# Two feed-forward down products: from eight block products a tile to seven, with the operand sums on GpSimd

## The chip, the cores and the metric

One Trainium2 chip, one of its cores. The metric is the device time of one launch in microseconds. All numbers are float32.

## The reference

A transformer of two blocks on 256 tokens of width 1024. The first block has two layers (one with a gated delta rule, one with sparse attention), each followed by a gated feed-forward part:

```
h   = rms_norm(x, norm_ffn_w[i])
u   = h @ ffn_w_up[i]                       # 1024 -> 2 x 2816, gate half and value half
g   = silu(causal_dwconv(u[gate], ffn_conv_w[i]) + ffn_conv_b[i]) * u[value]
x   = x + g @ ffn_w_down[i]                 # 2816 -> 1024: the down product
```

The second block has two layers with a mixer and a mixture of 32 experts. Before them, the modulations `silu(c) @ w_ada + b_ada` are computed: 24 chunks of 1024x512, spread through the first block.

## The kernel before

Each engine has its own instruction stream, written as one Python function, and the engines meet at semaphores (`wait_ge`, `then_inc`). Weights come through a ring `W` of six slots of 2 MB (128 partitions x 4096 values), filled in a fixed order by the SP queue: a fill waits until the slot's last reader has released it (`W.free`). PSUM is eight banks of 128x512 in two rings of four, `PA` and `PB`; a bank is taken in ring order, and the taker waits until its last reader has freed it.

The up product already uses seven block products in place of eight (`product(i, part)`, parts 1, 2, 7, 5, 6, 3, 4). Its weight sums run on VectorE (`up_sums`, `own_sums`), 128x1024 each, and write to the slot in place or to the ring `SUMS`.

The down product multiplies `G` (2816 features as 22 blocks of 128, each with 256 tokens) by the down weights. They come as six tiles: tile j > 0 holds blocks 4(j-1) to 4(j-1)+3, tile 0 the blocks 20 and 21, in the order `DOWNS = (1, 0, 2, 3, 4, 5)`. Function `down` (L764) keeps four sums in the four banks of `PA`, one for each half of the tokens (m) and each half of the columns (c), and adds every block with one 128x512 product: 16 products for a tile of four blocks. The last two tiles are one group, which finishes bank after bank, so that the residual `add_x` and the norm of the first half of the tokens start while TensorE does the second.

Between the groups TensorE does modulation sums `ada_sum(n)` (L804 on): one 128x512 product with a matrix of ones, into a bank of `PB`. It needs the chunk that VectorE has weighted and added up (`ada_chunk(n)`, L1817: one `tensor_scalar` and seven `scalar_tensor_tensor` of 128x512, all in the weight slot); VectorE then reads the bank (`ada_out(n)`). `ADA_DOWN` says which chunks stand behind which group: seven in layer 0, six in layer 1. In VectorE's stream chunk n comes ahead of the result n-1, and `add_x` follows the last result.

GpSimd issues a few DMAs in this part and does no arithmetic before the rotary embeddings of the second block.

Of the kernel before, what the change touches and what calls it, by code (L numbers as in the profile page):

```python
# [296 lines left out]
def build(nc, t, out):  # L297
# [34 lines left out]
    slots = [dma(f"w{i}") for i in range(NSLOT + 4)]  # L332
# [13 lines left out]
    def at(n, *shape):  # L346
        k = int(np.prod(shape))
        assert n + k <= ARENA, n + k
        return shaped(AR[:, n:n + k], shape)
# [41 lines left out]
    def tok(m):  # L391
        return slice(m * 128, m * 128 + 128)
# [126 lines left out]
    def blocks(place, kt, n):  # L519
        return place[:, 0:kt * n].rearrange("p (k n) -> p k n", k=kt)  # L520
# [21 lines left out]
    ADA_DOWN = [[(2,), (3, 4), (5, 6), (7, 8)], [(18,), (19,), (20, 21), (22, 23)]]  # L542
    ADA_NSA = [(), (9,), (10,), (11,), (12,)]
    ADA_MIX = {"v": 13, "aq": 14, "av": 15}
    DOWNS = (1, 0, 2, 3, 4, 5)

    def up_name(layer, i):
        return ("up", layer) + UPS[i]
# [154 lines left out]
    def tensor(e):  # L703
# [60 lines left out]
        def down(done, tag, srcs, lhs, between=(), then=None, ready=(), halfway=None):  # L764


            groups = [[x] for x in srcs[:-2]] + [srcs[-2:]]
            for n, group in enumerate(groups):
                held = [(weights(name, kt, 1024), k0, kt) for name, k0, kt in group]
                final = n == len(groups) - 1  # L770
                for m in range(2):
                    if n == 0 and m and halfway:
                        halfway()
                    for c in range(2):
                        if n == 0:
# [359 lines left out]
        def ffn(layer):  # L1135

            done, vect = sig("ffn_mm"), sig("ffn_v")
            tag = ("ffn", layer)

            def product(i, part):  # L1140
                name, nb = up_name(layer, i), up_blocks(i)
                a11, a12, a21, a22, total = up_tiles(layer, i)
                if part == 1:
                    bank(e, PB, ("p1", name))
                    place(name)
                    lhs, rhs, to = a11, HT[:, 0:4, tok(0)], (PB["p1", name], 0)
                    e.wait_ge(sig("norm_ha"), (tag, 0, 3))
                elif part == 2:
                    bank(e, PA, ("p26", name))
                    lhs, rhs, to = a12, HT[:, 4:8, tok(0)], (PA["p26", name], 0)  # L1150
                    e.wait_ge(sig("norm_ha"), (tag, 0, 7))
                elif part == 7:
                    bank(e, PA, ("p57", name))
                    lhs, rhs, to = a21, TS[2], (PA["p57", name], nb)
                    e.wait_ge(vect, ("t", layer, 2))
                    e.wait_ge(vect, ("s3", name))
                elif part == 5:
                    lhs, rhs, to = total, TS[0], (PA["p57", name], 0)
                    e.wait_ge(vect, ("t", layer, 0))
                    e.wait_ge(vect, ("s1", name))  # L1160
                elif part == 6:
                    lhs, rhs, to = a11, TS[1], (PA["p26", name], nb)
                    e.wait_ge(vect, ("t", layer, 1))
                    e.wait_ge(vect, ("s2", name))
                elif part == 3:
                    bank(e, PA, ("p34", name))
                    lhs, rhs, to = a12, HT[:, 4:8, tok(1)], (PA["p34", name], 0)
                    e.wait_ge(sig("norm_ha"), (tag, 1, 7))
                    e.wait_ge(vect, ("s4", name))
                else:  # L1170
# [12 lines left out]

            for i, part in ((0, 1), (0, 2), (1, 1)):
                product(i, part)
            norm_half(tag, 1)
            for i, part in ((1, 2), (2, 1), (0, 7), (0, 5), (0, 6), (0, 3), (0, 4), (1, 7), (1, 5), (1, 6)):
                product(i, part)
            PA.defer()
            product(1, 3)  # L1190
            product(1, 4)
            for i in range(2, 12):
                for part in (1, 2, 7, 5, 6, 3, 4)[i == 2:]:
                    product(i, part)
                if i - 1 in ADA_UP[layer]:
                    ada_sum(ADA_UP[layer][i - 1])

            srcs = [(("down", layer, j), 4 * (j - 1) if j else 20, 4 if j else 2) for j in DOWNS]
            ready = [(vect, ("val", layer, j - 1 if j else 5)) for j in DOWNS]
            down(done, tag, srcs, G, [lambda ns=ns: [ada_sum(n) for n in ns] for ns in ADA_DOWN[layer]],  # L1200
                 None if layer else "nsa", ready)

        def nsa():
            done, vect, act = sig("nsa_mm"), sig("nsa_v"), sig("nsa_a")
# [504 lines left out]
    def vector(v):  # L1709
# [107 lines left out]
        def ada_chunk(n):  # L1817
            done = sig("ada_v")
            name = ("ada", n)
            wt = blocks(W[name], 8, 512)  # L1820
            acc = wt[:, 0, :]
            v.wait_ge(slots[W.where[name]], name)
            v.wait_ge(sig("ada_a"), "c")
            v.tensor_scalar(acc, acc, CC[:, 0:1], None, MUL).then_inc(done)
            for k in range(1, 8):
                v.scalar_tensor_tensor(acc, wt[:, k, :], CC[:, k:k + 1], acc, MUL, ADD).then_inc(done, n if k == 7 else None)
# [299 lines left out]
        def ffn(layer):  # L2126
# [94 lines left out]
            last_results(11)  # L2221
            used(11)
            first, last = ADA_DOWN[layer][0][0], ADA_DOWN[layer][3][-1]
            for n in range(first, last + 2):
                if n <= last:
                    ada_chunk(n)
                if n > first:
                    ada_out(n - 1)
            for m in add_x(mm, tag, done):
# [1009 lines left out]
    def gpsimd(g):  # L3239
        def copies(dst, src, n):  # L3240
            return dst, src.broadcast_to([128, n])

        def ffn():

            g.wait_ge(sig("norm_mm"), (("ffn", 1), 1, 1))
            for layer in range(2):
                src = t["b_ada_2"][layer:layer + 1]
                g.dma_start(*copies(MG[:, layer * 1024:layer * 1024 + 1024], src[:, 2048:3072], 1024)).then_inc(dma("mg"))
                for half in range(2):
                    c = 5120 + 512 * half  # L3250
                    g.dma_start(experts_gate(layer)[64 * half:64 * half + 64, :], src[:, c:c + 512].broadcast_to([64, 512])).then_inc(dma("mg"))
            g.dma_start(*copies(MF[:, 0:1024], t["final_norm_w"], 1024)).then_inc(dma("fn"), "first")
# [54 lines left out]
                g.dma_start(*copies(MG[:, 0:1024], t["final_norm_g_2"], 1024)).then_inc(dma("fn"), "final")  # L3307

        small_weights()
        nsa()  # L3310
        ffn()
        for layer in range(2):
            mixers(layer)
            moe(layer)
# [88 lines left out]
```

## Time and profile before

| | us |
|---|---|
| runs, median (lowest to highest) | 2380.1 (2375.32 to 2380.3) |
| profiled execution, its own time | 2380.49 |
| span of that execution | 2378.7 |
| TensorE busy in the span | 2173.2 |
| VectorE busy | 1061.3 |
| ScalarE busy | 587.1 |
| GpSimd busy | 55.7 |

The span goes from the first to the last instruction in the trace. Busy times of different engines overlap, so they don't add up. A matrix product of 128x512 appears as two records in the trace, each with its load of weights; records overlap slightly, so the time of one is read from start to start. A bracket at the end of a row of the timeline tells how long the engine was idle before it and what released it.

### The profile page before, as it was taken

How to read it: one execution, taken by the hardware profiler on the slowest of the kernel's cores; microseconds unless marked ns; L12 is line 12 of the kernel's file. 1: busy time of each engine (PE TensorE's matmuls, PEld its weight loads, DVE VectorE, ACT ScalarE, POOL GpSimd, SP SyncE). 2: the span in 40 equal slices, each digit the busy share in tenths (PEclk: the TensorE clock that was granted, in tenths of full speed). 3: DMA queues.
4: the chain of work that ended last, by engine and by line, in shares of the span. 5: the costliest groups of instructions: out<-in, count | busy, mean ns of one | idle time of the engine just before them, and what ended most of it. 6: DMA issues, size and time to landing. Idle time of an engine off the chain costs nothing.

```text
span 2378.7 us, 32987 instructions
## 1 busy us (share of the span) xinstructions
PE 2173.2 (91%) x13520; PEld 1393.5 (59%) x13520; DVE 1061.3 (45%) x2378; ACT 587.1 (25%) x1321; POOL 55.7 (2%) x85
## 2 busy tenths in 40 slices
PE   8999999999999999999999987787899989988876
PEld 7777679847865996568743333333668744333332
DVE  4852568873443887575342222222335342222222
ACT  4332422001352310124521211111225331211111
POOL 0000000001000000002000000000011000000000
PEclk9999999999999999999999999999899999989999
DMA  8322244597921747837259999999852569999997
GB/s 310 106 77 90 107 168 153 211 376 193 321 74 38 282 172 275 302 119 257 112 242 415 427 427 427 428 428 427 305 175 107 212 286 427 428 427 427 428 427 323
DMA packets 144355, 650.47 MB, mean 273 GB/s; under 512 B 9067, under 2 KB 17547, under 8 KB 119617
## 3 DMA queue, kind: packets, MB, share of 16 engines
q1 hardware_dynamic: 141888, 641.46, 68.7%
q0 software_dynamic: 2304, 6.79, 1.2%
q8 instruction: 110, 1.80, 0.3%
q14 instruction: 53, 0.43, 0.1%
HBM read 646.91 MB, written 1.31 MB: 273 GB/s over the span
## 4 chain that ended last, share of the span: by engine, by line
PE 64%; DMA 21%; DVE 9%; ACT 4%; issue 1%; DVEq 0%; ACTq 0%
PE ps L106 61%; DMA wring<-in_w_gate 8%; DMA AR<-in_w_gate 4%; DMA wring<-in_w_up 4%; PE ps L109 3%; DVE wring L129 2%; DMA wring<-in_w_down 2%; DMA AR<-in_w_up 2%; DMA XB<-in_w_gate 2%; DVE AR L125 1%; ACT AR L115 1%; DVE AR L129 1%; ACT HT L115 1%; ACT L115 1%; DVE AR L120 1%
## 5 line engine op out<-in xcount | busy, mean ns | idle before, releaser
L106 PE MATMUL ps<-HT,wring 128*128 128x256 f32 (+1 forms) x3040 | 532.7, 333 | 9.3 <-DVE wring L125 4.0
L106 PEld LDWEIGHTS ps<-HT,wring 128*128 128x128 f32 x3040 | 470.4, 193 | 63.5 <-issue 12.4
L106 PE MATMUL ps<-wring,AR 128*32 128x512 f32 (+3 forms) x1312 | 337.3, 610 | 19.4 <-DMA wring<-in_w_down 10.5
L106 PE MATMUL ps<-wring,MN 128*32 128x512 f32 (+1 forms) x1376 | 219.0, 640 | 45.5 <-DMA wring<-in_w_gate 28.3
L115 ACT ACTIVATE AR<-ps 128x256 f32<-128x256 f32 (+6 forms) x235 | 89.0, 379 | 610.4 <-PE ps L106 567.5
L106 PEld LDWEIGHTS ps<-wring,AR 128*32 128x32 f32 (+1 forms) x1312 | 130.1, 149 | 178.2 <-issue 163.5
L141 DVE COPY HT<-ps 128x512 f32<-128x512 f32 x64 | 44.3, 692 | 416.0 <-PE ps L106 416.0
L106 PE MATMUL ps<-AR 64*64 64x64 f32 (+6 forms) x1848 | 163.5, 339 | 21.8 <-DMA AR<-in_w_down 8.9
L106 PEld LDWEIGHTS ps<-wring,MN 128*32 128x32 f32 (+1 forms) x1376 | 62.3, 122 | 194.5 <-issue 101.9
L115 ACT ACTIVATE HT<-ps 128x512 f32<-128x512 f32 x112 | 66.9, 597 | 349.8 <-PE ps L106 348.3
L125 DVE TENSOR_TENSOR AR<-ps,AR 128x512 f32<-128x512 f32 (+4 forms) x200 | 100.6, 503 | 117.8 <-PE ps L106 55.6
L106 PEld LDWEIGHTS ps<-CS,HT 128*128 128x128 f32 x1024 | 120.9, 192 | 54.9 <-issue 54.6
L106 PEld LDWEIGHTS ps<-AR 64*64 64x64 f32 (+4 forms) x1848 | 104.2, 147 | 57.7 <-issue 37.2
L106 PE MATMUL ps<-XN,wring 128*128 128x128 f32 x1056 | 130.1, 275 | 2.6 <-DVE wring L125 1.6
L129 DVE SCALAR_TENSOR_TENSOR wring<-wring,CC 128x512 f32<-128x512 f32 x168 | 126.3, 752 | 6.0
L106 PE MATMUL ps<-CS,HT 128*128 128x32 f32 x1024 | 128.1, 278 | 0.2 <-DVE HT L141 0.2
L106 PEld LDWEIGHTS ps<-XN,wring 128*128 128x128 f32 x1056 | 123.7, 192 | 3.4 <-DVE wring L125 2.0
L106 PE MATMUL ps<-XN,AR 128*128 128x128 f32 (+1 forms) x656 | 114.0, 414 | 1.0 <-DVE AR L125 1.0
L106 PE MATMUL ps<-AR,MN 128*32 128x512 f32 (+1 forms) x640 | 81.2, 610 | 23.1 <-DMA AR<-in_w_gate 13.7
L125 DVE TENSOR_TENSOR MN<-ps,AR 128x512 f32<-128x512 f32 x64 | 44.3, 692 | 129.1 <-PE ps L106 129.1
L115 ACT ACTIVATE AR<-AR,PV 128x256 f32<-128x256 f32 x104 | 52.8, 508 | 134.5 <-DVE AR L125 77.0
L106 PE MATMUL ps<-wring,HT 128*128 128x512 f32 (+3 forms) x256 | 85.5, 493 | 0.0
(183 smaller groups left out, 2066.2 us busy)
## 6 DMA issues: line engine op xcount, KB each, us to landing
wring<-in_w_up SPq DMA_DIRECT2D x40, 2048.0 KB, 42.1
wring<-in_w_gate SPq DMA_DIRECT2D x38, 2048.0 KB, 44.2
wring<-in_w_down SPq DMA_DIRECT2D x38, 2048.0 KB, 44.6
wring<-in_w_ada SPq DMA_DIRECT2D x24, 2048.0 KB, 10.2
wring<-in_ffn_w_up SPq DMA_DIRECT2D x20, 2048.0 KB, 8.3
AR<-in_w_down SPq DMA_DIRECT2D x20, 2048.0 KB, 46.0
AR<-in_w_gate SPq DMA_DIRECT2D x20, 2048.0 KB, 36.4
wring<-in_w_in SPq DMA_DIRECT2D x18, 2048.0 KB, 13.2
```

What stands on the lines that cost most here:

```text
L106: return Ins(self.eng and self.eng.matmul(out, lhs, rhs, start=start, stop=stop), None)
L109: return Ins(self.eng and self.eng.transpose(out, in_, ident), None)
L115: return Ins(self.eng and self.eng.activation(out, in_, func, **kw), self)
L120: return Ins(self.eng and self.eng.tensor_scalar(out, in_, s1, None, op0), self)
L125: return Ins(self.eng and self.eng.tensor_tensor(out, in0, in1, op), self)
L129: return Ins(self.eng and self.eng.scalar_tensor_tensor(out, in0, s, in1, op0, op1), self)
L141: return Ins(self.eng and self.eng.tensor_copy(out, in_), self)
```

## The change

Four of the six down tiles (1, 2, 3, 4) are now multiplied in the manner of the up product: a tile is seen as two by two blocks (two halves of the tokens by two pairs of feature blocks, times two pairs of feature blocks by two halves of the columns), and seven products of two 128x512 steps each replace eight. The seven sums run over all four tiles in seven banks, four of `PA` and three of `PB`, and are put together once, in `seven_sums` on VectorE, between the last chunk and its result. The fourth bank of `PB` alone serves the modulation sums in this time (`PB.order[:1]`). The last group is now tile 0 and tile 5 (six blocks) by the old function, and begins when the banks of parts 1, 2, 7 and 6 are free.

The sums of operands, four of 128x256 on `G` and four of 128x1024 on the weights for each tile, are made by GpSimd in a new function `down`, ahead of and behind its other work in the queue. Two of them overwrite their operand in the weight slot (`b12`, `b21`), one overwrites a part of `G` (`a21`). `T3`, `T2W` and `S124` are two places each for the others, so GpSimd may begin tile n when part 3 of tile n-2 is done.

The modulation sums are placed anew (`ADA_SEVEN`): at most one behind parts 7 or 4 of a tile, the last one in the middle of the last group.

```diff
-    DOWNS = (1, 0, 2, 3, 4, 5)
+    DOWNS = (1, 2, 3, 4, 0, 5)
+    SEVEN = (1, 2, 5, 7, 6, 3, 4)
+    ADA_SEVEN = [{(0, 4): 2, (1, 4): 3, (2, 7): 4, (2, 4): 5, (3, 7): 6, (3, 4): 7}, {(0, 4): 18, (1, 4): 19, (2, 4): 20, (3, 7): 21, (3, 4): 22}]
+    ADA_LAST = [8, 23]
...
-            down(done, tag, srcs, G, [lambda ns=ns: [ada_sum(n) for n in ns] for ns in ADA_DOWN[layer]],
-                 None if layer else "nsa", ready)
+            for n in range(4):
...
+                s1, s2, s4 = S124[n % 2]
+                pairs = {1: (a11, b11), 2: (a12, b21), 5: (s1, b12), 7: (a21, T3[n % 2]), 6: (s2, T2W[n % 2]), 3: (s4, b22), 4: (a22, b21)}
+                e.wait_ge(vect, ("val", layer, DOWNS[n] - 1))
+                for part in SEVEN:
+                    if n == 0:
+                        bank(e, PB if part in (5, 3, 4) else PA, (tag, "p", part))
+                    if part == 5:
+                        e.wait_ge(sums, (layer, n, "s4"))
+                        e.wait_ge(sums, (layer, n, "t1"))
+                    elif part == 6:
+                        e.wait_ge(sums, (layer, n, "t2"))
+                    elif part == 4:
+                        e.wait_ge(sums, (layer, n, "t4"))
+                    ps = (PB if part in (5, 3, 4) else PA)[tag, "p", part]
+                    lhs, rhs = pairs[part]
+                    for k in range(2):
+                        ins = e.matmul(ps[:, :], lhs[:, k, :], rhs[:, k, :], n == 0 and k == 0, n == 3 and k == 1)
+                    ins.then_inc(done, (tag, "p", n, part))
+                    if part == 4:
+                        W.free(name, (done, (tag, "p", n, 4)))
+                        if n == 0:
+                            PB.order = PB.order[:1]
+                    if (n, part) in ADA_SEVEN[layer]:
+                        ada_sum(ADA_SEVEN[layer][n, part])
...
+            def seven_sums():
...
+                v.wait_ge(mm, (tag, "p", 3, 2))
+                v.tensor_copy(t[0], p(1)).then_inc(done, (tag, "p", 1))
...
+                v.tensor_tensor(x(0, 0), p(2), x(0, 0), ADD).then_inc(done, (tag, "p", 2))
+                v.tensor_tensor(x(0, 0), x(0, 0), t[0], ADD).then_inc(done)
+                v.wait_ge(mm, (tag, "p", 3, 6))
+                v.tensor_tensor(t[0], p(6), t[0], ADD).then_inc(done, (tag, "p", 6))
+                v.tensor_tensor(t[1], p(7), t[0], ADD).then_inc(done, (tag, "p", 7))
+                v.tensor_tensor(t[0], p(5), t[0], ADD).then_inc(done)
+                v.tensor_tensor(t[2], p(5), t[1], ADD).then_inc(done, (tag, "p", 5))
+                v.wait_ge(mm, (tag, "p", 3, 4))
+                v.tensor_tensor(t[0], p(3), t[0], ADD).then_inc(done, (tag, "p", 3))
+                v.tensor_tensor(t[1], t[1], p(4), SUB).then_inc(done, (tag, "p", 4))
+                for (m, c), y in (((0, 1), t[0]), ((1, 0), t[1]), ((1, 1), t[2])):
+                    v.tensor_tensor(x(m, c), x(m, c), y, ADD).then_inc(done)
...
+        def down(layer):
...
+                g.wait_ge(sig("ffn_v"), ("val", layer, DOWNS[n] - 1))
+                if n > 1:
+                    g.wait_ge(mm, (tag, "p", n - 2, 3))
+                g.tensor_tensor(s1, a21, a22, ADD).then_inc(done)
+                g.tensor_tensor(a21, a11, a21, SUB).then_inc(done)
+                g.tensor_tensor(s2, s1, a11, SUB).then_inc(done)
+                g.tensor_tensor(s4, a12, s2, SUB).then_inc(done, (layer, n, "s4"))
+                g.wait_ge(slots[W.where[name]], name)
+                g.tensor_tensor(t3, b22, b12, SUB).then_inc(done)
+                g.tensor_tensor(b12, b12, b11, SUB).then_inc(done, (layer, n, "t1"))
+                if n < 2:
+                    g.wait_ge(mm, (up_name(layer, 10 + n), 5))
+                    g.wait_ge(sig("ffn_v"), ("s2", up_name(layer, 10 + n)))
+                g.tensor_tensor(t2, b22, b12, SUB).then_inc(done, (layer, n, "t2"))
+                g.wait_ge(mm, (tag, "p", n, 2))
+                g.tensor_tensor(b21, t2, b21, SUB).then_inc(done, (layer, n, "t4"))
...
         small_weights()
+        down(0)
         nsa()
         ffn()
+        down(1)
```

## Rows read from the trace of the kernel before

**Rows 1.** The page's head and busy times (engine, us, share, instructions).

```profile
span 2378.7 us, 32987 instructions
PE 2173.2 (91%) x13520; PEld 1393.5 (59%) x13520; DVE 1061.3 (45%) x2378; ACT 587.1 (25%) x1321; POOL 55.7 (2%) x85
```

**Rows 2.** Stretches: bounds, length, busy per engine, granted clock, DMA share, GB/s.

```profile
463.00:548.00 85.00, 84.28 (x210) 37.79 (x209) 59.58 (x99) 4.68 (x13) 0.00 (x0) 1.00 0.87 325
...
916.00:998.00 82.00, 82.00 (x201) 36.84 (x200) 48.89 (x80) 2.34 (x7) 0.00 (x0) 1.00 0.84 314
...
1400.00:1680.00 280.00, 224.86 (x1520) 88.54 (x1512) 58.56 (x147) 42.14 (x93) 0.00 (x0) 0.93 1.00 424
```

**Rows 3.** Waits of the SP queue from 1000 to 1700 us: total, times, longest.

```profile
SPq L101 <- PE ps L106: 543.7, 99, 39.2
```

**Rows 4.** Timeline of TensorE, layer 0: start, us, what [idle before, releaser].

```profile
462.75 13.90 PE L106 MATMUL ps<-wring,AR 128*128 128x512 f32 x32
476.49 1.02 PE L106 MATMUL ps<-wring,CS 128*128 128x512 f32 x2
...
485.71 1.12 PE L106 MATMUL ps<-wring,CS 128*128 128x512 f32 x2 [0.47 <-DVE wring L129]
...
546.70 4.63 PE L106 MATMUL ps<-HT,wring 128*128 128x128 f32 x40
```

**Rows 5.** Groups of VectorE, 462.7 to 548 us: busy us, mean ns, idle before.

```profile
L129 DVE SCALAR_TENSOR_TENSOR wring<-wring,CC 128x512 f32<-128x512 f32 x49 | 36.8, 752 | 1.7
```

**Rows 6.** Timeline of VectorE, layer 0: first chunk's start, last chunk, first finished bank.

```profile
465.52 0.49 DVE L120 TENSOR_SCALAR wring<-wring,CC 128x512 f32<-128x512 f32 x1
...
511.86 5.48 DVE L129 SCALAR_TENSOR_TENSOR wring<-wring,CC 128x512 f32<-128x512 f32 x7
...
525.42 0.69 DVE L125 TENSOR_TENSOR XB<-ps,XB 128x512 f32<-128x512 f32 x1 [4.42 <-PE ps L106]
```

**Rows 7.** Timelines of VectorE and TensorE, layer 1.

```profile
953.49 0.69 DVE L125 TENSOR_TENSOR AR<-ps,AR 128x512 f32<-128x512 f32 x1 [7.79 <-PE ps L106]
...
961.71 5.48 DVE L129 SCALAR_TENSOR_TENSOR wring<-wring,CC 128x512 f32<-128x512 f32 x7
...
969.59 27.63 PE L106 MATMUL ps<-wring,AR 128*128 128x512 f32 x64
```

**Rows 8.** Groups of GpSimd over the whole span, shapes apart.

```profile
L125 POOL TENSOR_TENSOR XN<-AR,CS 128x160 f32<-128x160 f32 x16 | 8.3, 521 | 1.3
L125 POOL TENSOR_TENSOR AR<-AR,CS 128x640 f32<-128x640 f32 x4 | 6.2, 1538 | 0.3
L125 POOL TENSOR_TENSOR XN<-AR,XN 128x256 f32<-128x256 f32 x8 | 5.8, 726 | 0.6
...
L125 POOL TENSOR_TENSOR XN<-AR,XN 128x128 f32<-128x128 f32 x4 | 1.8, 455 | 0.3
```

**Rows 9.** Timelines of VectorE and GpSimd in the rotary embeddings, 1092 to 1107 us.

```profile
1092.56 0.29 DVE L133 CUSTOM_DVE_ANT_0 AR<-ps,CS 128x128 f32<-128x128 f32 x1
...
1092.61 1.54 POOL L125 TENSOR_TENSOR AR<-AR,CS 128x640 f32<-128x640 f32 x1
...
1092.89 1.28 DVE L125 TENSOR_TENSOR SM<-SM 128x4 f32<-128x4 f32 x1
...
1097.68 0.16 DVE L125 TENSOR_TENSOR SM<-SM 128x4 f32<-128x4 f32 x1
...
1097.70 1.27 POOL L125 TENSOR_TENSOR AR<-AR,RB 128x512 f32<-128x512 f32 x1
...
1098.09 1.04 DVE L120 TENSOR_SCALAR AR<-AR,SM 128x256 f32<-128x256 f32 x1
...
1106.13 0.35 DVE L120 TENSOR_SCALAR AR<-AR,SM 128x256 f32<-128x256 f32 x1
```

**Rows 10.** Up product's tail, layer 0: a TensorE wait; VectorE's waits, 440 to 548 us.

```profile
449.38 2.05 PE L106 MATMUL ps<-XN,wring 128*128 128x128 f32 x16 [1.26 <-DVE wring L125]
...
DVE AR L125 <- PE ps L106: 1.7, 2, 0.9
```

More of the change, by code:

```diff
@@ L544, in build, with down_quarters @@
     ADA_MIX = {"v": 13, "aq": 14, "av": 15}
-    DOWNS = (1, 0, 2, 3, 4, 5)
+    DOWNS = (1, 2, 3, 4, 0, 5)
+    SEVEN = (1, 2, 5, 7, 6, 3, 4)
+    ADA_SEVEN = [{(0, 4): 2, (1, 4): 3, (2, 7): 4, (2, 4): 5, (3, 7): 6, (3, 4): 7}, {(0, 4): 18, (1, 4): 19, (2, 4): 20, (3, 7): 21, (3, 4): 22}]
+    ADA_LAST = [8, 23]
+    T3 = [at(3072, 2, 512), MF[:, 1024:2048].rearrange("p (a b) -> p a b", a=2)]
+    T2W = [at(4096, 2, 512), at(5120, 2, 512)]
+    S124 = [[at(c + 256 * j, 2, 128) for j in range(3)] for c in (9776, 6656)]
+    def down_quarters(layer, n):
+        wt = blocks(W["down", layer, DOWNS[n]], 4, 1024)
+        k0 = 4 * (DOWNS[n] - 1)
+        a = [[G[:, k0 + 2 * k:k0 + 2 * k + 2, tok(m)] for k in range(2)] for m in range(2)]
+        b = [[wt[:, 2 * k:2 * k + 2, 512 * c:512 * c + 512] for c in range(2)] for k in range(2)]
+        return a, b
     def up_name(layer, i):
@@ L1196, in ffn @@
                     ada_sum(ADA_UP[layer][i - 1])
-            srcs = [(("down", layer, j), 4 * (j - 1) if j else 20, 4 if j else 2) for j in DOWNS]
-            ready = [(vect, ("val", layer, j - 1 if j else 5)) for j in DOWNS]
-            down(done, tag, srcs, G, [lambda ns=ns: [ada_sum(n) for n in ns] for ns in ADA_DOWN[layer]],
-                 None if layer else "nsa", ready)
+            rest = list(PB.order)
+            sums = sig("down_g")
+            for n in range(4):
+                name = ("down", layer, DOWNS[n])
+                place(name)
+                (a11, a12), (a21, a22) = down_quarters(layer, n)[0]
+                (b11, b12), (b21, b22) = down_quarters(layer, n)[1]
+                s1, s2, s4 = S124[n % 2]
[22 more added lines that the diff above has]
+                        ada_sum(ADA_SEVEN[layer][n, part])
@@ L1203, in nsa, with last_sum @@
+            def last_sum():
+                ada_sum(ADA_LAST[layer])
+                turns = (7, 6)[layer] % 4
+                PB.order = rest[turns:] + rest[:turns]
+            down(done, tag, [(("down", layer, 0), 20, 2), (("down", layer, 5), 16, 4)], G, (), None if layer else "nsa",
+                 [(vect, ("val", layer, 5)), (vect, ("val", layer, 4))], last_sum)
         def nsa():
@@ L2223, in ffn, with used_up @@
             first, last = ADA_DOWN[layer][0][0], ADA_DOWN[layer][3][-1]
+            def seven_sums():
+                t = [XF[:, 512 * j:512 * j + 512] for j in range(4)]
+                x = lambda m, c: X[:, m, 512 * c:512 * c + 512]
+                p = lambda part: (PB if part in (5, 3, 4) else PA)[tag, "p", part][:, :]
+                def used_up(part):
+                    (PB if part in (5, 3, 4) else PA).free((tag, "p", part), (done, (tag, "p", part)))
+                v.wait_ge(mm, (tag, "p", 3, 2))
+                v.tensor_copy(t[0], p(1)).then_inc(done, (tag, "p", 1))
+                used_up(1)
+                v.tensor_tensor(x(0, 0), p(2), x(0, 0), ADD).then_inc(done, (tag, "p", 2))
+                used_up(2)
+                v.tensor_tensor(x(0, 0), x(0, 0), t[0], ADD).then_inc(done)
+                v.wait_ge(mm, (tag, "p", 3, 6))
+                v.tensor_tensor(t[0], p(6), t[0], ADD).then_inc(done, (tag, "p", 6))
+                used_up(6)
+                v.tensor_tensor(t[1], p(7), t[0], ADD).then_inc(done, (tag, "p", 7))
+                used_up(7)
+                v.tensor_tensor(t[0], p(5), t[0], ADD).then_inc(done)
+                v.tensor_tensor(t[2], p(5), t[1], ADD).then_inc(done, (tag, "p", 5))
+                used_up(5)
+                v.wait_ge(mm, (tag, "p", 3, 4))
+                v.tensor_tensor(t[0], p(3), t[0], ADD).then_inc(done, (tag, "p", 3))
+                used_up(3)
+                v.tensor_tensor(t[1], t[1], p(4), SUB).then_inc(done, (tag, "p", 4))
+                used_up(4)
+                for (m, c), y in (((0, 1), t[0]), ((1, 0), t[1]), ((1, 1), t[2])):
+                    v.tensor_tensor(x(m, c), x(m, c), y, ADD).then_inc(done)
             for n in range(first, last + 2):
@@ L2226, in ffn @@
                     ada_chunk(n)
+                if n == last:
+                    seven_sums()
                 if n > first:
@@ L3241, in copies @@
             return dst, src.broadcast_to([128, n])
+        def down(layer):
+            done, mm = sig("down_g"), sig("ffn_mm")
+            tag = ("ffn", layer)
+            for n in range(4):
+                name = ("down", layer, DOWNS[n])
+                (a11, a12), (a21, a22) = down_quarters(layer, n)[0]
+                (b11, b12), (b21, b22) = down_quarters(layer, n)[1]
+                s1, s2, s4 = S124[n % 2]
+                t3, t2 = T3[n % 2], T2W[n % 2]
+                g.wait_ge(sig("ffn_v"), ("val", layer, DOWNS[n] - 1))
[14 more added lines that the diff above has]
+                g.tensor_tensor(b21, t2, b21, SUB).then_inc(done, (layer, n, "t4"))
         def ffn():
```

## The prediction, made before the changed kernel ran

> **What bounds the kernel now.** I read the page first [rows 1]: TensorE is busy for 91% of 2378.7 us, VectorE for 45%, GpSimd for 2%. An average says nothing about the two down products, so the next view is the table of stretches [rows 2]. From 463 to 548 us (the down product of layer 0) TensorE works 84.28 of 85.00 us at the full clock (1.00, the 2.4 GHz level); from 916 to 998 us (layer 1) 82.00 of 82.00. In these two stretches every product taken away shortens the program, as long as nothing else is late. The expert stage after 1400 us is different: DMA share 1.00. But its transfers are issued when TensorE frees slots: of the SP queue's waits, 543.7 us end with TensorE [rows 3]. A shift in the feed-forward part therefore passes to the end one for one, in either direction.
>
> Then TensorE's order of time in layer 0 [rows 4]. One tile of the down weights is 32 records from 462.75 to 476.49, so 13.74 us; it holds 16 products of 128x512 (two records each), so 0.859 us a product. At 485.71 TensorE waits 0.47 us for VectorE: a modulation sum whose chunk was not ready. VectorE is the second thing to read [rows 5]: between 462.7 and 548 it runs seven modulation chunks, each one TENSOR_SCALAR of 0.49 us and seven SCALAR_TENSOR_TENSOR of 0.75 us (49 in all). The first chunk begins at 465.52, the last ends at 511.86 + 5.48 = 517.34, and only from 521.0 on does VectorE wait, 4.42 us, for the first finished bank at 525.42 [rows 6]. So VectorE is nearly as full as TensorE here. In layer 1 it has six chunks and a long wait (7.79 us before 953.49), so there is more slack [rows 7].
>
> **What is removed.** A tile of four 128-row blocks goes from 16 products to 14. Four tiles a layer, two layers: 16 products x 0.859 = 13.7 us, 6.9 a layer. The modulation sums stay: one 128x512 product each, 0.86 us.
>
> **What is added on GpSimd.** For each tile four sums of 128x256 and four of 128x1024, all with both inputs in SBUF. The forms it ran before [rows 8]: 128x128 in 455 ns and 128x256 in 726, a slope of 2.12 ns an element; 128x160 in 521 and 128x640 in 1538, 2.12 again. A 1024-wide sum is then 0.726 + 768 x 0.00212 = 2.35 us. A tile costs 4 x 0.73 + 4 x 2.35 = 12.3 us, with eight gaps of 0.07 us 12.9. A tile on TensorE is now 14 x 0.859 = 12.0 us plus one or two modulation sums, 12.9 to 13.7. The last sum of a tile waits for part 2 of that tile (its input is overwritten), and part 5 of the next tile wants four short sums and the third long one from then: 2.42 + 4 x 0.80 + 2 x 2.42 = 10.5 us in one period of 12.9 to 13.7. Undisturbed, GpSimd just keeps up.
>
> **What it costs VectorE.** This decides. The trace has GpSimd and VectorE side by side in one place, the rotary sums near 1090 us [rows 9]. A TENSOR_TENSOR of 128x4 with both inputs in SBUF takes 0.16 us at 1097.68. At 1092.89 the same takes 1.28 us and ends at 1094.17, when the GpSimd operation that began at 1092.61 for 1.54 us has ended (1094.15). A TENSOR_SCALAR of 128x256 takes 0.35 us at 1106.13 and 1.04 at 1098.09, until 0.16 us after the end of GpSimd's (1097.70 + 1.27 = 1098.97). An operation with one of its inputs in PSUM is not stretched (0.29 us at 1092.56, beside the same GpSimd sum). So a VectorE operation that reads two SBUF operands, or a TENSOR_SCALAR from SBUF, stands still until the running GpSimd operation ends; some 0.15 to 0.2 us of its fixed part is hidden in the wait. A modulation chunk consists of nothing but such operations. They are each under 0.8 us and GpSimd's are up to 2.35, so every GpSimd sum lets about one VectorE operation pass and stops the next.
>
> The price: after the up product ends, 25 GpSimd sums are left (the last of tile 0, eight each of three tiles): 13 x 2.35 + 12 x 0.73 = 39.3 us, less 25 x 0.15 = 35.5 us. In layer 0 VectorE has 51.8 us of work between 465.5 and 517.3, seven chunks of 6.1 us in it, a share of 0.82: it loses 29.1 us. Before that, in the tail of the up product, three long sums of tile 0 fall on VectorE's chunk and weight sums: 3 x 2.2 = 6.6 us, less 1.7 us that VectorE itself waits for TensorE there, 4.9. TensorE already waits 1.26 us for VectorE at 449.38 [rows 10]. The four short sums of tile 0 run earlier in the up product, 4 x 0.58 = 2.3 at most; I put 1.5 a layer.
>
> **What is late next.** The last group of TensorE (24 products with no splitting) needs the banks of parts 1, 2, 7 and 6, which VectorE empties only after the last chunk. In the trace of before that chunk ends at 517.34 and one copy of 0.69 us more would free the first bank at 518.0. With the loss: 518.0 + 4.9 + 29.1 = 552.0. Then 24 products and one modulation sum, 25 x 0.859 = 21.5 us, to 573.5. Before, the stage ended at 546.70 [rows 4]. Layer 0: +26.8 us. In layer 1 the last chunk ends at 961.71 + 5.48 = 967.19 [rows 7], after the wait of 7.79 us, which a late VectorE doesn't have; the first bank would be free at 967.19 + 0.69 - 7.79 = 960.1. Six chunks of 6.1 and four results of 0.72 (0.69 and a gap) make a share of 0.93 there: 960.1 + 4.9 + 33.0 = 998.0, plus 21.5 = 1019.5, against 969.59 + 27.63 = 997.2: +22.3. With 3.0 for the short sums that is +52.1 us. I take 42, some 10 less, because the shares are means: a GpSimd sum that begins while VectorE waits for TensorE or reads PSUM costs less than one in a chunk, and the modulation results wait for TensorE more than before.
>
> **Bounds.** The trace shows only VectorE standing still [rows 9]. No row shows GpSimd waiting: its 128x160 sums keep a mean of 0.52 us, with short VectorE operations beside some of them [rows 8]. If a GpSimd sum starts while a VectorE operation runs, up to 0.75 us of it are beside that operation and cost nothing: 25 x 0.75 x 0.82 = 15.4 less in layer 0, 17.4 in layer 1, 33 in all, so 52 - 33 = +19. By the Trainium skill (SBUF — State Buffer, "Who interferes with whom") the block works both ways, whoever starts first holds the shared pair of ports for the whole instruction. By that rule the lower bound falls away and the sum stays near +42 to +52. In the other direction, nothing of VectorE's fixed part hidden: 25 x 0.15 x 0.87 x 2 = 6.5 more, +59. And TensorE gets waits of several us between groups; where it has waits, in the expert stage, the mean granted clock is 0.93 [rows 2]. At 0.93 the 70 us of products a layer cost 5 more each: +69.
>
> **Edits at almost no cost.** The 12 operations that put the seven banks together are 12 x 0.72 = 8.7 us on VectorE. They fall beside the last group (21.5 us), and the bank of part 7 comes four operations (2.9 us) after that of part 2 while TensorE wants it 11.2 us after the first. Without that cover they would cost their 8.7. Seven of the eight banks stay held, so the modulation sums share one and each waits for the result before it, on VectorE (51.8 - 42.7) / 5 = 1.8 us. The order of the down tiles moves the 1 MB tile to the end; the SP queue's transfers are the same, and the stretch has a DMA share of 0.87, so earlier need is possible but tight.
>
> **The rivals.**
> 1. *Faster.* VectorE isn't held in the long sums as in the short ones, or it gets its turns between GpSimd's. Then TensorE's products decide. The bank must be free at 546.7 - 21.5 = 525.2 in layer 0 and 975.7 in layer 1 for no loss, against 518.0 and 960.1 undisturbed. So the break-even is 7.2 us over 25 sums, 0.29 us a sum, in layer 0 and 15.6 us, 0.62 a sum, in layer 1: for both together about 0.45. I expect 1.2 to 1.4. Fully undisturbed layer 0 still waits some 2 us for the bank: -5 and -7, 2368 us. For it: VectorE's operations in PSUM aren't touched. Against: every two-input operation that meets a GpSimd sum ends with it [rows 9].
> 2. *Mildly slower: GpSimd is the bound instead.* VectorE wins the turns, GpSimd's eight sums a tile each wait 0.6 us: 12.9 + 4.8 = 17.7 us a tile against 13.3. Three tiles, 13 us, less 3 us of slack and the 6.9 saved: +3 to +6 a layer, 2386 to 2392. Against: nothing shows GpSimd waiting.
> 3. *No change: transfers take it.* The tile's weights are now wanted by GpSimd, half a tile before TensorE. At 0.87 of DMA share over 85 us, 74 us of transfers must fit in 78. If each tile is late by 1.7 us the gain is gone: 2380. Against: TensorE waits for no DMA in the stretch.
>
> **How the numbers follow.** The profiled run took 2380.5 us, its span is 2378.7; the three runs shown have the median 2380.1, so the sum is made against 2380.5 and moves nothing by that. Forecast 2380.5 + 42 = 2422. Chances: VectorE held up 0.73, rival 2 0.10, rival 1 0.12, rival 3 0.05. 0.2% is 4.8 us, about what a measurement can tell from no change: faster 0.12, same 0.06, slower 0.82. The range leaves out rival 1, the mildest cases and the far end with the lowered clock: 2388 to 2446.
>
> **What would show it.** The 128x1024 sums on GpSimd near 2.4 us, or 2.9 if they wait too. VectorE's SCALAR_TENSOR_TENSOR of 0.75 us at a mean of 1.2 us or more between 463 and 560 us. TensorE with waits on VectorE for the modulation sums and for the bank at the start of the last group, each layer's stretch longer by 15 to 27 us, though its products are 6.9 us fewer. Wrong if these means stay at 0.75 us: then the time falls to about 2368.

## The result and the profile after

| | us | ratio to before, 95% interval |
|---|---|---|
| predicted | 2422.0 (2388 to 2446) | |
| after, median of 5 runs (2422.55 to 2424.15) | 2423.1 | 1.0188 [1.0176, 1.0199] |
| before, median of 5 runs (2375.32 to 2382.68) | 2380.1 | |
| span of the profiled execution after | 2421.5 | |

Chips differ by a few us: the kernel before had medians of 2376.2 to 2380.1 beside the runs below, so each experiment is given as its ratio to the kernel before, measured beside it.

First the page. TensorE has 32 records fewer, the 16 products taken away, and yet the program is 43 us longer:

```profile
span 2421.5 us, 33046 instructions
PE 2170.2 (90%) x13488; PEld 1390.9 (57%) x13488; DVE 1142.8 (47%) x2402; ACT 587.1 (24%) x1321; POOL 174.9 (7%) x149
L129 DVE SCALAR_TENSOR_TENSOR wring<-wring,CC 128x512 f32<-128x512 f32 x168 | 170.1, 1013 | 6.0
```

TensorE's busy time fell by 3.0 us only [rows 1], where the products taken away are worth 13.7 at the full clock; the granted clock further down tells why. The third line is the modulation chunks of the whole program: the same 168 operations take 170.1 us in place of 126.3 (168 of 752 ns [rows 5]), 43.8 us more.

Then the stretches that hold the two down stages, in the columns of [rows 2]:

```profile
463.00:573.00 110.00, 85.73 (x206) 37.87 (x205) 95.98 (x113) 4.68 (x13) 45.80 (x25) 0.89 0.69 252
935.00:1040.00 105.00, 89.82 (x261) 44.35 (x261) 91.68 (x99) 3.80 (x9) 46.53 (x26) 0.93 0.69 250
```

VectorE (the third of the engines) now works 96 of 110 us in layer 0 and TensorE (the first) idles 24 of them; before, TensorE idled 0.7 of 85 us. The granted clock, 1.00 before, is 0.89 and 0.93.

GpSimd's groups by form (busy us, mean ns | idle before) tell how long its sums took:

```profile
L125 POOL TENSOR_TENSOR AR<-AR 128x256 f32<-128x256 f32 x32 | 36.3, 1135 | 351.7 <-DVE AR L125 349.3
L125 POOL TENSOR_TENSOR AR<-wring 128x1024 f32<-128x1024 f32 x12 | 31.4, 2616 | 69.1 <-DMA wring<-in_ffn_w_down 50.5 <-DVE wring L125 17.7
L125 POOL TENSOR_TENSOR wring<-AR,wring 128x1024 f32<-128x1024 f32 x8 | 21.3, 2664 | 47.4 <-PE ps L106 46.8
...
L125 POOL TENSOR_TENSOR XN<-AR,XN 128x256 f32<-128x256 f32 x8 | 5.8, 726 | 0.6
```

The last row is the old rotary sum, still 726 ns; the new sums of the same size take 1135 on average. So GpSimd waits as well, on average 0.41 us in a short sum and some 0.26 in these long ones (undisturbed they take 2.35 and 2.40, experiment 7).

VectorE's timeline in layer 0 shows the chunks (each row is the seven SCALAR_TENSOR_TENSOR of one) and the copy that frees the first bank. Undisturbed such a row is 5.48 us [rows 6]. The last two of the seven, at 534.08 and 542.08, are left out here and take just that:

```profile
468.95 10.84 DVE L129 SCALAR_TENSOR_TENSOR wring<-wring,CC 128x512 f32<-128x512 f32 x7
482.31 10.51 DVE L129 SCALAR_TENSOR_TENSOR wring<-wring,CC 128x512 f32<-128x512 f32 x7
498.65 12.79 DVE L129 SCALAR_TENSOR_TENSOR wring<-wring,CC 128x512 f32<-128x512 f32 x7
516.38 5.47 DVE L129 SCALAR_TENSOR_TENSOR wring<-wring,CC 128x512 f32<-128x512 f32 x7
524.19 7.51 DVE L129 SCALAR_TENSOR_TENSOR wring<-wring,CC 128x512 f32<-128x512 f32 x7
...
547.66 0.69 DVE L141 COPY XN<-ps 128x512 f32<-128x512 f32 x1
```

The groups by form from 463 to 548 us have the means. SCALAR_TENSOR_TENSOR is at 1155 ns (752 before [rows 5]), and the chunks' TENSOR_SCALAR stands still too, at 1299 ns where it takes 0.49 us undisturbed [rows 6]:

```profile
L129 DVE SCALAR_TENSOR_TENSOR wring<-wring,CC 128x512 f32<-128x512 f32 x49 | 56.6, 1155 | 1.7
L120 DVE TENSOR_SCALAR wring<-wring,CC 128x512 f32<-128x512 f32 x7 | 9.1, 1299 | 0.8
```

TensorE's timeline has the matching waits in brackets, and then the end of each layer's stage (layer 0 at 574.02, layer 1 at 1042.50):

```profile
479.94 1.10 PE L106 MATMUL ps<-wring,CS 128*128 128x512 f32 x2 [2.10 <-DVE wring L129]
...
513.91 2.08 PE L106 MATMUL ps<-wring,CS 128*128 128x512 f32 x2 [9.75 <-DVE MC L125]
...
548.50 12.77 PE L106 MATMUL ps<-wring,AR 128*128 128x512 f32 x24 [5.87 <-DVE XN L141]
...
574.02 2.17 PE L106 MATMUL ps<-HT,wring 128*128 128x128 f32 x18
...
1042.50 1.04 PE L109 MATMUL ps<-CS,XN 128*128 128x128 f32 x8
```

The wait of 9.75 us is the third modulation sum: it needs the shared bank, and the bank needs the result of the sum before, which stands behind a slow chunk on VectorE (498.65, 12.79 us). Layer 0 ends 27.3 us later than before (546.70 [rows 4]), layer 1 45.4 later (997.1), so 18.1 us are its own. The span grew by 42.8, 2.6 less.

The timelines split this further. The stage itself, from its first down product to its end, takes 108.4 us in place of 83.9 in layer 0 (it begins at 465.66) and 95.2 in place of 80.7 in layer 1: 24.4 and 14.5 us more. The rest lies ahead of the stages, in the tails of the up product: 3.6 us in layer 1, and 5.1 in layer 0. The clock times show only 2.9 of these 5.1, because this execution was already 2.2 us ahead of that of before when GpSimd's first sum began at 404.18 (the run of 32 products ahead of it begins at 399.62 in place of 401.79).

The last group has a loss of its own. It begins behind the wait for the bank, and here are its first twelve products and what follows, in both layers (stretches, columns as above):

```profile
548.50:561.10 12.60, 12.60 (x24) 5.48 (x25) 9.22 (x15) 0.00 (x0) 0.00 (x0) 0.82 0.34 124
561.10:574.00 12.90, 12.37 (x35) 5.67 (x34) 6.12 (x14) 4.68 (x13) 0.00 (x0) 1.00 0.47 164
1017.90:1031.30 13.40, 13.37 (x24) 5.76 (x25) 8.20 (x12) 0.00 (x0) 0.00 (x0) 0.77 0.50 182
```

Twelve products at the full clock are 12 x 0.859 = 10.3 us. They take 12.6 at a mean clock of 0.82 and 13.4 at 0.77: after its waits TensorE works part of this time at the lower level (1.2 GHz), and 2.3 and 3.1 us are lost. Behind them the clock is back at 1.00 (second row).

Last, the block itself, at the end of layer 0's up product. First VectorE's timeline, then GpSimd's:

```profile
447.43 1.23 DVE L125 TENSOR_TENSOR wring<-AR,wring 128x1024 f32<-128x1024 f32 x1
448.68 1.22 DVE L125 TENSOR_TENSOR AR<-AR 128x1024 f32<-128x1024 f32 x1
450.01 3.18 DVE L125 TENSOR_TENSOR wring<-wring 128x1024 f32<-128x1024 f32 x1
```

```profile
448.78 3.32 POOL L125 TENSOR_TENSOR AR<-wring 128x1024 f32<-128x1024 f32 x1 [8.84 <-DVE wring L125]
```

VectorE begins at 448.68, GpSimd 0.10 us behind it. GpSimd's sum takes 3.32 us: 2.35 and about the 1 us that VectorE's ran on. VectorE's next one begins at 450.01, takes 3.18 us in place of 1.23 and ends at 453.19, 1.1 us after GpSimd's (452.10). Whoever comes second stands still, in either direction.

### The profile page after: what moved, and what is told of

It reads as the page before. It is cut to its first block, busy times and chain, and to the rows that moved or that the text cites. A ratio compares the mean times of both kernels' runs of the same rounds, so it can differ in the third digit from the quotient of the medians.

```text
span 2421.5 us, 33046 instructions
## 1 busy us (share of the span) xinstructions
PE 2170.2 (90%) x13488; PEld 1390.9 (57%) x13488; DVE 1142.8 (47%) x2402; ACT 587.1 (24%) x1321; POOL 174.9 (7%) x149
## 4 chain that ended last, share of the span: by engine, by line
PE 58%; DMA 21%; DVE 15%; ACT 4%; issue 2%; DVEq 0%; ACTq 0%
PE ps L106 56%; DMA wring<-in_w_gate 7%; DVE wring L129 6%; DMA wring<-in_w_up 6%; DMA wring<-in_w_down 4%; PE ps L109 3%; DVE AR L125 2%; DMA XB<-in_w_gate 2%; DMA AR<-in_w_gate 2%; DVE AR L129 1%; DVE wring L125 1%; ACT AR L115 1%; DVE wring L120 1%; ACT HT L115 1%; DVE AR L120 1%
## 5 line engine op out<-in xcount | busy, mean ns | idle before, releaser
L106 PE MATMUL ps<-wring,AR 128*32 128x512 f32 (+3 forms) x1216 | 299.6, 597 | 31.1 <-DMA wring<-in_w_down 13.3
L106 PEld LDWEIGHTS ps<-wring,AR 128*32 128x32 f32 (+1 forms) x1216 | 113.9, 146 | 171.8 <-issue 154.0
L106 PE MATMUL ps<-AR 64*64 64x64 f32 (+7 forms) x1896 | 186.6, 347 | 21.7 <-DMA AR<-in_w_down 8.7
L129 DVE SCALAR_TENSOR_TENSOR wring<-wring,CC 128x512 f32<-128x512 f32 x168 | 170.1, 1013 | 6.0
L106 PEld LDWEIGHTS ps<-AR 64*64 64x64 f32 (+4 forms) x1896 | 112.3, 147 | 71.3 <-issue 49.6
```

The lines of the kernel that those rows point to most:

```text
L106: return Ins(self.eng and self.eng.matmul(out, lhs, rhs, start=start, stop=stop), None)
L129: return Ins(self.eng and self.eng.scalar_tensor_tensor(out, in0, s, in1, op0, op1), self)
```

## The experiments

Theory A is that of the prediction: GpSimd's sums hold up VectorE's operations on two SBUF operands, and VectorE's delay is the loss. The rivals: the seven-product form itself (banks, order) costs the time, GpSimd is too slow, or VectorE simply has more to do.

**1. Without the sums.** `down` on GpSimd is left out, and the parts multiply unsummed blocks. All else is the changed kernel.

```diff
-    pairs = {... 5: (s1, b12), 7: (a21, T3[n % 2]), 6: (s2, T2W[n % 2]), 3: (s4, b22), ...}
+    pairs = {... 5: (a11, b12), 7: (a21, b12), 6: (a21, b22), 3: (a12, b22), ...}
...
-        down(0)
...
-        down(1)
```

> The changed kernel with GpSimd's operand sums left out: the seven parts multiply unsummed blocks, so the output is not the reference's; everything else (seven banks, the one bank for the modulation sums, the putting together, the order of the tiles) stays. Theory A (VectorE's two-input operations collide with GpSimd's sums): VectorE's SCALAR_TENSOR_TENSOR goes back to 752 ns and the time falls to 2366 to 2371 us, 10 to 14 below the kernel before. Theory B (the seven held banks and the chain sum - result - sum through one bank are what is late): the time stays above 2400.

Measured: 2369.96 us, ratio 0.9974 [0.9961, 0.9987]. VectorE's group is back at its old mean, and TensorE has one wait over 1 us in layer 0's stage (second row, TensorE's timeline). The third row is the stretch behind that wait:

```profile
L129 DVE SCALAR_TENSOR_TENSOR wring<-wring,CC 128x512 f32<-128x512 f32 x168 | 126.3, 752 | 6.0
...
518.86 13.51 PE L106 MATMUL ps<-wring,AR 128*128 128x512 f32 x24 [5.10 <-DVE XN L141]
...
518.80:532.30 13.50, 13.44 (x25) 5.84 (x26) 9.28 (x15) 0.00 (x0) 0.00 (x0) 0.78 0.64 235
...
486.33 0.70 DVE L125 TENSOR_TENSOR ps<-ps,CS 128x512 f32<-128x512 f32 x1 [3.05 <-PE ps L106]
```

So the form without its sums is worth 0.0026 x 2380 = 6 us (3 to 9 by the interval), not the 13.7 of the products. In layer 0 TensorE waits 5.1 us for the first bank, and the twelve products behind the wait take 3.0 us more than 10.3 (518.86 to 532.21), at a mean clock around 0.78. No GpSimd sum holds up VectorE here: it waits itself 3.05 us for TensorE (last row, VectorE's timeline), because the second modulation sum is placed later than before (24.9 us behind the stage's start in place of 21.5). In layer 1 TensorE waits 1.77 us for the bank. By the trace layer 0's stage is 0.8 us longer than before (84.7 against 83.9) and layer 1's 4.9 shorter (75.8 against 80.7): all of the gain is in layer 1, 4.1 us in sum. The other (1.0188 - 0.9974) x 2380 = 51 us lie with the sums.

**2. Without the chunks' work.** The sums stay, and in the two down stages 78 of the chunks' SCALAR_TENSOR_TENSOR are left out.

```diff
-            for k in range(1, 8):
+            inside = 2 <= n <= 8 or n >= 18
+            for k in range(7 if inside else 1, 8):
```

> The changed kernel with GpSimd's sums, but of each modulation chunk in the two down products (2 to 8 and 18 to 23) only the first and the last of eight operations on VectorE; 78 operations of 0.75 us are left out. Theory A: the collisions go with them; 2366 to 2374 us. Theory C (GpSimd itself is too slow for TensorE, whatever VectorE does): 2385 or more, with TensorE waiting for GpSimd.

Measured: 2372.43 us, ratio 0.9987 [0.9977, 0.9996]. TensorE has no wait over 0.6 us in layer 0's stage. GpSimd's long sums have means of 2.34 to 2.53 us, and the short ones of 0.93. GpSimd with all its sums keeps up with TensorE. Both stages are now shorter than before, by 7.5 and 6.9 us; most of this is lost again ahead of them, where the sums of tile 0 still meet VectorE's (4.6 us of waits in layer 0's tail, 1.8 before). Only the two kinds of work together cost.

**3. Sums without use.** The kernel before, sixteen products a tile, with as many GpSimd sums of the same sizes on spare places; TensorE waits for the last only at the stage's end.

```diff
+            e.wait_ge(sig("down_g"), (layer, 3))
...
+                for s in (s1, s2, s4, s1):
+                    g.tensor_tensor(s, s, s, SUB).then_inc(done)
...
+                g.tensor_tensor(t3, t3, t3, SUB).then_inc(done)
+                g.tensor_tensor(t3, t3, t3, SUB).then_inc(done)
...
```

> The kernel before, down products of eight and four banks for the modulation sums, and beside them the same number and shapes of GpSimd sums at about the same times, on spare places, with nobody waiting for them until the stage has ended. Theory A: VectorE loses the same time, the modulation sums come late, 2405 to 2435 us. Theory B: nothing of the new bank order is here, so it stays at 2380.

Measured: 2417.22 us, ratio 1.0170 [1.0153, 1.0188]. Neither the seven banks nor the single bank for the modulation sums is there, nor does TensorE read any sum within the stage; the sums alone make the kernel 1.7% slower. TensorE waits for VectorE's chunks, 17.4 us in four waits in layer 0 (waits from 463 to 575 us: total, times, longest):

```profile
L129 DVE SCALAR_TENSOR_TENSOR wring<-wring,CC 128x512 f32<-128x512 f32 x168 | 159.0, 946 | 6.0
...
PE ps L106 <- DVE wring L129: 17.4, 4, 7.0
```

The mean is 946 ns and not 1013, in line with shorter sums: these read one place twice, and their long ones have a mean of 2.11 us with all their delays, where those of the changed kernel have 2.45 to 2.66.

**4. The sums on VectorE.** GpSimd does nothing; VectorE makes the same sums between its chunks, in a written order.

```diff
+            def tile_sums(n):
...
+                v.tensor_tensor(s1, a21, a22, ADD).then_inc(dsum)
...
+            plan = ("S0 c0 T0 S1 c1 o0 T1 S2 c2 o1 T2 c3 o2 S3 c4 o3 T3 c5 o4 c6",
+                    "S0 c0 T0 S1 c1 o0 T1 S2 c2 o1 T2 S3 c3 o2 T3 c4 o3 c5")[layer]
```

> The changed kernel with the operand sums on VectorE, between the chunks; GpSimd does none. A 1024-wide sum takes VectorE 1.26 us and a 256-wide one 0.45, so 6.8 us a tile, 27 a layer, 54 in all, close to what VectorE lost to GpSimd by the trace of the changed kernel (168 SCALAR_TENSOR_TENSOR 43.8 us longer, and more in the single-input ones). Theory A: within 15 us of the changed kernel, 2408 to 2435. Theory B or C: the same as without sums or far below, under 2395, since GpSimd's pace is gone.

Measured: 2419.1 us, ratio 1.0174 [1.0154, 1.0195], as slow as the changed kernel within their intervals. The chunks are at 752 ns again, but a tile's sums take 4 x 1.23 + 4 x 0.45 = 6.7 us of VectorE's own time. Here the two engines, holding each other up, did no more than VectorE alone. Taken by itself this run would fit the third rival too (VectorE simply has more to do); experiment 3 (slow, with VectorE's work of before) and experiment 5 (fast, with that of the changed kernel) are against it.

**5. Chunks in the bank.** The chunk accumulates in the PSUM bank that its sum will use, so that each operation has one operand in SBUF and one in PSUM; only the last one writes to SBUF. Since one bank is left, the result of chunk n-1 comes before chunk n. Chunk 8 moves behind the down stage, and the modulation sums are placed anew.

```diff
-        def ada_chunk(n):
+        def ada_chunk(n, in_bank=False):
...
+            if in_bank:
+                after(v, PB, ("ada", n))
+                ps = PB["ada", n][:, :]
+                v.tensor_scalar(ps, acc, CC[:, 0:1], None, MUL).then_inc(done)
+                for k in range(1, 8):
+                    v.scalar_tensor_tensor(acc if k == 7 else ps, wt[:, k, :], CC[:, k:k + 1], ps, MUL, ADD).then_inc(done, n if k == 7 else None)
+                return
             v.tensor_scalar(acc, acc, CC[:, 0:1], None, MUL).then_inc(done)
...
+                ada_chunk(n, True)
...
```

> The changed kernel, with each chunk in the two down products accumulated in the PSUM bank that its modulation sum uses, so that no operation of it reads two SBUF operands; result n-1 comes ahead of chunk n, the modulation sums are placed where the chunks should be ready, and chunk 8 goes to the next stage. By theory A the collisions vanish although GpSimd does all its sums: SCALAR_TENSOR_TENSOR at 750 ns in these stretches, 2366 to 2374 us. If PSUM doesn't help (VectorE is held whatever it reads), it stays above 2410.

Measured: 2384.97 us, ratio 1.0034 [1.0022, 1.0046]. It is 37 us faster than the changed kernel, but slower than before and 11 us above the upper end of what was expected. The mechanism is as expected. VectorE's and GpSimd's timelines in layer 0:

```profile
470.50 0.75 DVE L120 TENSOR_SCALAR ps<-wring,CC 128x512 f32<-128x512 f32 x1
471.29 4.71 DVE L129 SCALAR_TENSOR_TENSOR ps<-wring,CC,ps 128x512 f32<-128x512 f32 x6
476.04 0.75 DVE L129 SCALAR_TENSOR_TENSOR wring<-wring,CC,ps 128x512 f32<-128x512 f32 x1
```

```profile
471.41 2.40 POOL L125 TENSOR_TENSOR wring<-AR,wring 128x1024 f32<-128x1024 f32 x1 [17.18 <-PE ps L106]
473.89 3.13 POOL L125 TENSOR_TENSOR AR<-AR 128x256 f32<-128x256 f32 x4
```

Six operations in 4.71 us beside two kinds of GpSimd sums, and neither side is stretched. What the expectation left out stands elsewhere: the tails of the up product, where tile 0's sums still meet VectorE's own sums, and a wait for chunk 7 that now comes after the seven banks' sums:

```profile
450.82 2.87 PE L106 MATMUL ps<-XN,wring 128*128 128x128 f32 x16 [2.05 <-DVE wring L125]
455.37 3.63 PE L106 MATMUL ps<-HT,wring 128*128 128x128 f32 x16 [1.68 <-DVE wring L125]
...
536.84 1.70 PE L106 MATMUL ps<-wring,CS 128*128 128x512 f32 x2 [3.55 <-DVE wring L129]
```

**6. The plan alone.** The same plan as in 5, with the chunks in SBUF as before (`ada_chunk(n, False)`).

> The same order and places as the kernel with the chunks in the bank, but the chunks accumulate in SBUF as before. Theory A: the collisions remain and the result-before-chunk order adds waits: 2415 to 2450 us. Theory B (the order of sums and results was the fault, and the new places cure it): below 2390.

Measured: 2425.56 us, ratio 1.0204 [1.0186, 1.0223]. The plan has no part in the gain of 5: the two kernels differ in that one argument, and the place of the accumulator alone makes 40.6 us.

**7. Tile 0's sums out of the way.** On top of 5. GpSimd makes tile 0's weight sums first and its short sums and `t2` only when VectorE's last long weight sums of the up product are through, beside operations that read a bank. TensorE takes the sum of chunk 7 later.

```diff
+                if n == 0:
+                    g.wait_ge(slots[W.where[name]], name)
+                    g.tensor_tensor(t3, b22, b12, SUB).then_inc(done)
+                    g.tensor_tensor(b12, b12, b11, SUB).then_inc(done, (layer, n, "t1"))
+                    g.wait_ge(sig("ffn_v"), ("s3", up_name(layer, 11)))
                 g.wait_ge(sig("ffn_v"), ("val", layer, DOWNS[n] - 1))
```

> The kernel whose chunks accumulate in their own bank measured 2385.0 us, some 15 us above the 2370 us of the kernel without any sums. Its trace shows where these lie: TensorE's waits for VectorE's sums in the two up tails (2.05 and 1.68 us in layer 0, 2.17 and 1.19 in layer 1, where the kernel before waits 1.26 and 0.54), four VectorE sums of 1.56 to 3.18 us instead of 1.23 there, one wait of 3.55 us for chunk 7 in layer 0's stage, and a later start of transfers after chunk 8 was moved behind the stage. Two edits: GpSimd does tile 0's sums of weights first and its short sums and t2 only after VectorE's sums for up tile 11 are issued, beside VectorE's operations that read a bank (a window of 5.6 us for 5.5 us of sums), and TensorE takes the sum of chunk 7 later. Theory (the block between operations with both operands in SBUF): every VectorE sum of the up tails is back at 1.23 us, each up tail gives back 2 to 3 us, the stage of layer 0 another 1.5 to 3.5 us: 2377 us (2373 to 2380), so the half products end at or a little under the kernel before. Rival (VectorE itself has too much to do in the tails, whoever stands beside it): the waits in the up tails stay above 3 us in sum and the time stays at 2383 to 2386 us.

Measured: 2376.52 us (12 runs) against 2376.21 (17 runs), ratio 1.0006 [0.9996, 1.0015]: no difference from before. Against 5 it gave back (1.0034 - 1.0006) x 2380 = 6.7 us, of the 8 expected. GpSimd's sums are at their undisturbed time (groups by form), and the wait of 3.55 us for chunk 7 is not there any more; a wait of 2.18 us for VectorE stays in layer 0's tail:

```profile
L125 POOL TENSOR_TENSOR AR<-wring 128x1024 f32<-128x1024 f32 x12 | 28.2, 2353 | 408.9 <-DMA wring<-in_ffn_w_down 407.7
L125 POOL TENSOR_TENSOR AR<-AR 128x256 f32<-128x256 f32 x32 | 23.3, 728 | 28.2 <-DVE wring L125 25.8
```

**8. That order in the changed kernel.** The edit of GpSimd's queue from 7 alone, chunks in SBUF.

> The changed kernel with one edit: GpSimd's order for tile 0 is sums of weights first, and the four short sums and t2 only after VectorE's sums for up tile 11, so that they stand beside VectorE's operations that read a bank. Chunks stay in SBUF. Theory: only the up tails' part comes back, 2 to 3 us a layer of the 43 us: 2418 us (2415 to 2421). Rival (the up tails' collisions are hidden behind the later waits for the chunks, which then only begin sooner): under 1 us in all, 2422 to 2425 us, with the stages' own waits longer by what the tails gave back.

Measured: 2416.0 us, ratio 1.0167 [1.0152, 1.0182]; against the 1.0188 of the changed kernel that is some 5 us, both layers together. The two intervals overlap a little (1.0176 to 1.0182), so by the times alone this speaks for the theory (2 to 3 us a layer) more than it proves it. The traces agree with it: layer 0's stage begins 2.9 us sooner than in the changed kernel (462.80 against 465.66), and the time between the two stages is 2.3 us shorter. TensorE's waits for VectorE in layer 0's stage have not grown: 22.4 us in six waits, 23.8 in seven in the changed kernel.

## Why the prediction was right

The time (2422.0 against 2423.1) and the mechanism hold: GpSimd's sums stop VectorE, and VectorE's delay reaches TensorE. That the time fits to 1 us is in part luck, as the terms show:

- **Removed products.** 32 records are gone, 0.86 us each pair. What they are worth undisturbed I had as 12 us (rival 1, 2368); experiment 1 gives about 6. The mis-sized term is layer 0's wait for the first bank, some 2 us in the prediction, 5.1 measured: the sum let VectorE's chunks follow each other as before, but with the new places of the modulation sums VectorE waits 3.05 us for TensorE. The lower clock behind that wait (3.0 us) and layer 1's wait for the bank (1.77) were no terms at all.
- **GpSimd's sums.** Predicted 2.35 and 0.73 us: 2.353 and 0.728 in experiment 7, where nothing stands in their way; in the changed kernel means up to 2.66, and 1.14. The Trainium skill (SBUF — State Buffer, "Who interferes with whom") has the block in both directions, and the trace agrees (448.78, 3.32 us). The sum had VectorE alone as the one that waits; GpSimd's own delays had no price, and no wait on GpSimd shows in TensorE's timeline.
- **VectorE's loss.** Predicted 29.1 us in layer 0. The seven rows of chunks sum to 58.1 us against 7 x 5.48 = 38.4, 19.7 more, and their TENSOR_SCALAR to 9.1 against 3.4, 5.7 more. Two small operations of the results, 1.53 and 0.65 us in place of 0.16, add 1.9: 27.3 us, a little under the price. With the first chunk 2.9 us later than before (468.43 against 465.52) the bank should come at 518.0 + 2.9 + 27.3 = 548.2. It was free at 548.35, so nothing else delayed it; predicted 552.0. The sign that was named, a mean of 1.2 us or more, was just missed (1155 ns).
- **What is late next.** The wait that ends on that bank is there in both layers, 5.87 and 5.32 us. It is a poor sign of the theory, though: without any GpSimd sum it is 5.10 in layer 0 (experiment 1). What the sums add in layer 0 comes earlier, at the modulation sums: six waits of 17.9 us (9.75 in one of them) where experiment 1 has none, since each needs the single bank. The prediction's chain led through the last bank only. In layer 0 that comes to the same end, because VectorE never pauses between its first chunk and the bank, and TensorE is behind it at both places.
- **The last group.** 25 products, predicted 21.5 us. Layer 0: 574.02 - 548.50 = 25.5, of which 2.3 are the clock and 1.7 the transposes and their wait in the middle (567.1 to 568.86), which the sum left out. Here two errors cancelled, which is luck: the bank came 3.7 us sooner, the group took 4.0 longer, and the end is 574.0 where 573.5 was forecast. The prediction kept the clock for the upper bound alone (+69); it belonged into the sum, for the products behind a wait.
- **Layer 1.** Less the 27.3 us that it started late, the bank came at 1017.93 - 27.3 = 990.6, predicted 998.0, 7.4 us too late. About these make it up: VectorE's loss was 28.1 us where 33.0 was priced (seven-operation rows 24.0 and TENSOR_SCALAR 4.1 longer than before), the tail cost 3.6 and not 4.9, and two more waits for TensorE of before (0.85 and 0.94 us) are gone like the one of 7.79. The lower clock in the last group took 3.1 us of this back. The end is 18.1 us further behind than layer 0's, predicted 22.3.
- **The sum.** 52.1 us by its steps, taken down to 42. Measured +42.8 of span: 27.3 + 18.1 - 2.6. By its parts the stages cost 24.4 + 14.5 = 38.9 us, where the steps had 39.3, and the tails 5.1 + 3.6 = 8.7, where they had 12.8: 47.6 in all. So some 4 of the 10 us taken off have a counterpart, in the tails. The rest of the agreement is luck: the 2.2 us that this execution was ahead earlier on and the 2.6 made up behind the stages (47.6 - 2.2 - 2.6 = 42.8) are no effect that the prediction names. Experiment 1, whose kernel is the same behind the stages, is 3.5 us shorter there than the kernel before, so differences of this size between single executions mean nothing.
- **The tails.** Predicted 4.9 and 1.5 us a layer, 12.8 in all, measured 8.7. Experiment 8 takes most of these collisions away and gives back some 5. The price per collision was about right (1.95 us in the row shown); that tile 0's long sums would meet three long VectorE operations was not. In layer 0 two of them (435.16 and 437.59) ran mostly beside operations that read a bank, and held up only one small operation (1.01 us in place of 0.16).
- **Rival 2** had GpSimd as the bound because VectorE delays it. GpSimd is delayed, as it says, but TensorE's waits of layer 0 in the changed kernel name VectorE alone (its weight loads wait 0.7 us for GpSimd in all), and experiment 2 shows that GpSimd's pace by itself is enough. **Rival 3** (transfers) has nothing for it: no wait of TensorE in that stage ends with a DMA, and the DMA share fell to 0.69.

Why 7 stays at the time of before, when experiment 1 reaches 0.9974, was only read in the trace, not tested. Its two stages are 4.4 and 5.6 us shorter than before (79.5 and 75.1 us), but the time between them is 8.2 us longer. Chunk 8 is worked on later there, so its slot is free later, and the waits on the memory tile's transfer behind it grow: ScalarE's on `in_mem` is 6.9 us against 2.8 before, TensorE's on VectorE's copies 6.2 against 2.8. These 3.4 us don't explain all of the 8.2.

## What to carry to other kernels

GpSimd is no free engine beside a VectorE that works from SBUF: before moving sums to it, count how full VectorE is in that stage and with which operands, and price each GpSimd sum at its full length, times the share of the time that VectorE is so at work (29.1 us by this price in layer 0, 27.3 measured). The sums fit where VectorE reads one operand from PSUM, or where it waits. An accumulator put in PSUM gave back 40 us here with no other change, so try the place of the operands before the order of the work; and price a saved product by what waits behind it (here about 6 us of 13.7 remained). None of the versions that do the whole work was faster than the kernel before: the best, experiment 7, is level with it.

## What the runs showed of the hardware

- SCALAR_TENSOR_TENSOR of 128x512 with its accumulator in PSUM takes 0.78 us from start to start (six in 4.71), in SBUF 0.78 as well (seven in 5.48): the move costs nothing when undisturbed. TENSOR_SCALAR is dearer with its result in PSUM: 0.75 us (470.50 in experiment 5), against 0.49 within SBUF [rows 6].
- A GpSimd sum that reads the same place twice takes 1.89 us for 1024 elements where nothing holds it up (experiment 3, the two from 438.19 on; its mean of 2.11 holds delays), one of two places 2.35 (experiment 7).
- A wait of TensorE cost more than its length: behind waits of 5.1 to 5.9 us the next twelve products took 2.3 to 3.1 us more than at the full clock, at a mean granted clock of 0.77 to 0.82.
